# Early value blocks fetched ahead of the first expert row, and six expert chains written as loops

## The chip, the cores and the metric

The kernel runs on one core of a Trainium2 chip. Its time is the device time of one execution in microseconds (us). The core has TensorE (PE; its weight loads are shown as PEld), VectorE (DVE), ScalarE (ACT), GpSimd (POOL) and SyncE (SP), which run their own instruction streams and meet at semaphores, and 16 DMA engines that serve queues filled by SP, ACT and POOL.

## What is computed

Two transformer blocks over 16 meta tokens and 256 real tokens of width 1024. The part that the change touches is the expert layer of the first block:

```python
q = (t @ w_peer_q).reshape(T, PEER_HEADS, 2, PEER_HALF)
s1 = jnp.einsum('thd,hkd->thk', q[:, :, 0], sub_keys1)      # 8 heads, 128 keys
s2 = jnp.einsum('thd,hkd->thk', q[:, :, 1], sub_keys2)
v1, i1 = lax.top_k(s1, PEER_TOPK)                            # 16 of 128, twice
v2, i2 = lax.top_k(s2, PEER_TOPK)
sc, pos = lax.top_k(cand, PEER_TOPK)                         # 16 of the sums v1 + v2
gates = jax.nn.softmax(sc, axis=-1)
...
act = jax.nn.gelu(jnp.einsum('nkd,nd->nk', expert_u[e], xt), approximate=False)
y = jnp.einsum('nk,nkd->nd', g * act, expert_v[e])
```

Every token takes 8 heads times 16 experts, and every expert is a row of 2 x 1024 floats (u and v). The second block begins with projections of the normalised result; its values are `a @ w_in_2[:, values]`.

## The kernel before, in words

Weights come as a stream of 206 blocks of 128 x 1024 floats (512 KB). SP loads block b into slot b % 4 of `ring` as soon as block b - 4 has been split (L432 to L445). ACT rounds a block into `w_hi` (`split_hi`, L356 to L363), DVE writes the rest into `w_lo` (`split_lo`, L365 to L372), and PE multiplies with both. The blocks around the change are 24 to 31 (`w_out`), 32 to 39 (`w_peer_q`), 40 to 47 (`w_in_2_values_0`: the values of the second block's first 128 real tokens and of the meta tokens, here the "early value blocks") and 48 and on (`w_in_2_features`), which wait for the last dot product.

The expert layer runs as 256 rows (SLOTS), in 16 chains of 16 (a chain is one head for one half of the tokens). For row n, with one token on each of the 128 partitions:

- POOL gathers 128 expert rows of 8 KB by index into buffer n % 8 of `gathered` (L510 to L517), 1 MB in all. It waits until PE has used row n - 8 (`row_used`).
- DVE multiplies the u half with the token and sums (`dot`, L2147 to L2159), into a `product` buffer.
- ACT makes gelu, coefficient and a diagonal matrix of it (`coefficient`, L1446 to L1458).
- PE multiplies the diagonal with the v half and adds into PSUM (`add_row`, L938 to L947).

Between the dots DVE works out the experts of later chains: `route_step` has 18 steps for a chain (`STEPS`), and `route_to` spreads them, three for each of the first six rows and about 18/16 for each row after. ACT's `top_exp` and DVE's `gates` make the softmax weights of a chain at its row 12 and rows 14 and 15 of the chain before. The whole row stage is written out, without loops, on every engine; later stages have loops (PE: L1078, L1152, L1156; ACT and DVE have short ones).

Ahead of row 0 ACT's order is: `w_out` and `w_peer_q` splits between `query_hi` pieces, `take_query(0)`, the first scores, further queries and scores, `gain_tokens`, the root, `top_exp(0)`. DVE's is: `route_step(0, ...)`, `first_experts` (which releases the first gathers), and so on. Blocks 40 and 41 are split at rows 48 and 52 (`AHEAD_AT`), blocks 42 to 47 every ten rows from row 170 (`EARLY_AT`), where their tiles are multiplied. As the ring has four slots, block 40 is loaded when block 36 is split, 41 to 43 at rows 0, 1 and 3, 44 and 45 at rows 49 and 53, 46 and 47 at rows 174 and 184.

Of the kernel before, what the change touches and what calls it, by code (L numbers as in the profile page):

```python
# [108 lines left out]
EARLY_AT, EARLY_STEP = SLOTS // 2 + 42, 10  # L109
BANK = [g % 2 if g < TILE0["w_out"] or 0 <= g - TILE0["w_peer_q"] < 8 else g % 2 + 2 if 0 <= g - TILE0["w_in_2_values_0"] < 8  # L110
# [14 lines left out]
def build(nc, stream, rows_dram, small_dram, keys_dram, kiwi_dram, gain_dram, x_dram, gain_rows_dram, meta_2_dram, out_dram):  # L125
    with ExitStack() as ctx:
# [13 lines left out]
        x_hi = sb("x_hi", [P, C * T], F32R)  # L140
# [99 lines left out]
        for name, n in (("qp", PH * REAL), ("sc", CHAINS * 2 * NKEYS), ("v", 2 * TOPK), ("cand", SPREAD),  # L240
                        ("tv", SLOTS), ("gate", SLOTS), ("sum", CHAINS), ("rsum", CHAINS), ("ix", 2 * TOPK),
                        ("pos", TOPK), ("hi", TOPK), ("lo", TOPK), ("af", TOPK), ("bf", TOPK), ("row1", TOPK),
                        ("eq1", TOPK * TOPK), ("eq2", TOPK * TOPK), ("i1", TOPK), ("i2", TOPK),
                        ("expert", SLOTS), ("late", 4), ("dot", SLOTS), ("gelu", SLOTS), ("coef", SLOTS),
                        ("diag", DIAGS * P), ("product", 2 * D), ("scaled", D), ("normed", D), ("stats", 24)):
            route[name] = work[:, base:base + n]
            base += n
        assert base <= WORK, base
        peer_x = (tokens_of(x_peer, REAL), tokens_of(x_lo, REAL))
# [4 lines left out]
        late = route["late"].bitcast(U32)  # L254
        halves_dram = rows_dram.rearrange("e (h n) -> (e h) n", h=2)

# [27 lines left out]
        sq_late = work[:, ROWS * ROW:ROWS * ROW + C * T]  # L284

# [34 lines left out]
        row_landed = [sem(f"row_landed{i}") for i in range(ROWS)]  # L320
        late_chosen, late_landed = sem("late_chosen"), [sem(f"late_landed{i}") for i in range(2)]
# [9 lines left out]
        norm1_landed = sem("norm1_landed")  # L331
# [23 lines left out]
        def split_hi(act, b, turn=None):  # L355

            if b >= BLOCKS:
                return
            t, k = (0, b % RING) if turn is None else (turn, b % RING)
            act.wait_ge(landed[k], t * 16 + 16 * (b // RING + 1))  # L360
            if turn is not None or b >= RING:
                act.wait_ge(block_begun, t * RING + (b - RING + 2))
            nc.scalar.activation(w_hi[:, k, :], ring[:, k, :], ACT.Copy).then_inc(w_hi_ready, 1)  # L363

        def split_lo(dve, b, turn=None):  # L365
# [5 lines left out]
            nc.vector.tensor_tensor(w_lo[:, k, :], ring[:, k, :], w_hi[:, k, :].bitcast(F32),  # L371
# [46 lines left out]
        def _(sp):  # L418
            at = SMALL["norm1"][0]
            sp.dma_start(norm1_gain[:, :], small_dram[:, at:at + C]).then_inc(norm1_landed, 16)  # L420
# [10 lines left out]
            for first, end in ((1, late), (late + 2, BLOCKS // RING)):  # L431
# [5 lines left out]
                if first == 1:  # L437
                    for b in range(late * RING, (late + 2) * RING):
# [113 lines left out]
        AHEAD_AT = {8: 48, 9: 52}  # L552
# [615 lines left out]
        def _(act):  # L1168
# [185 lines left out]

            def query_hi(n):
# [21 lines left out]
            query_hi(0)  # L1377
            split_hi(act, wo + 5)
# [39 lines left out]
            def top_exp(c):  # L1418

                act.wait_ge(tops_shifted, c + 1)  # L1420
                act.wait_ge(peer_rooted, 1)
                g = route["gate"][:, TOPK * c:TOPK * c + TOPK]
                t = c // PH
                a(g, g, ACT.Exp, scale=peer_root[:, t:t + 1],
                  accum_out=route["sum"][:, c:c + 1]).then_inc(tops_exp, 1)

            take_query(0)
            act.wait_ge(first_scores_ready, 1)
# [13 lines left out]
            top_exp(0)  # L1442
# [3 lines left out]
            def coefficient(n):  # L1446

                act.wait_ge(dotted, n + 1)
                t = n // (SLOTS // 2)
                link(a(route["gelu"][:, n:n + 1], route["dot"][:, n:n + 1], ACT.Gelu, scale=peer_root[:, t:t + 1]))  # L1450
                if n % TOPK == 0:
                    act.wait_ge(gates_ready, n // TOPK + 1)
                link(a(route["coef"][:, n:n + 1], route["gelu"][:, n:n + 1], ACT.Copy,  # L1453
# [1171 lines left out]
```

## Time and profile before

| | |
|---|---|
| median of three runs | 1331.97 us (1330.75 to 1331.97) |
| the profiled execution | 1331.13 us, of which 1329.4 us are the span of the trace |
| mean granted TensorE clock | 0.99 |
| busy: PE, DVE, ACT, POOL | 89%, 67%, 51%, 20% of the span |
| DMA | 382.25 MB, mean 288 GB/s over the span |

A profile page gives the busy time of each engine, the span in 40 equal slices (33 us each; a digit is a busy share in tenths), the DMA queues, and the chain of waits followed back from the last instruction. A row of a group or of the timeline names the line of the kernel, the engine, what is written from what, the count and the time; in brackets or behind the bar stands the idle time before it and who ended it. The row stage is the stretch from 191.6 us (first dot) to 837.3 us (end of the last).

### The profile page before, as it was taken

The numbers are of one execution on the slowest core, as the hardware profiler recorded it, in microseconds if no ns is written. First come the engines' busy times: TensorE is split into PE (matmuls) and PEld (weight loads), VectorE is DVE, ScalarE is ACT, GpSimd is POOL, SyncE is SP. The second block draws the span as 40 slices with busy tenths as digits, with TensorE's granted clock in tenths as the row PEclk, the third lists the DMA queues.
The fourth block names the chain that finished last, engine by engine and source line by source line (L and its number), as shares of the span: only waits on it lengthen the run. The fifth ranks groups of instructions, "written<-read, shape, count | busy, mean of one in ns | idle before, by whom it ended". The sixth has DMA issues, their size and how long they took to land.

```text
span 1329.4 us, 19028 instructions
## 1 busy us (share of the span) xinstructions
PE 1187.2 (89%) x6314; PEld 835.7 (63%) x6314; DVE 886.1 (67%) x1939; ACT 683.1 (51%) x1483; POOL 270.9 (20%) x307
## 2 busy tenths in 40 slices
PE   8899989987787878788778878999999999999998
PEld 6898874532222223233333323799999999999986
DVE  6664688666666667776766654666877657666664
ACT  6555655545444345554455544534456675444454
POOL 4000023433333333343333333000000020000000
PEclk9899999999999999999999999999999999999999
DMA  6331389999999999999999999535565355555563
GB/s 240 118 114 64 113 324 419 421 421 420 422 421 422 421 422 420 384 415 422 420 421 421 421 422 413 192 126 190 166 217 188 127 169 181 174 175 183 178 214 101
DMA packets 68939, 382.25 MB, mean 288 GB/s; under 512 B 7792, under 2 KB 7920, under 8 KB 36224
## 3 DMA queue, kind: packets, MB, share of 16 engines
q0 software_dynamic: 37152, 268.45, 48.8%
q1 hardware_dynamic: 31424, 112.05, 25.7%
q10 hardware_dynamic: 288, 0.82, 0.2%
q8 instruction: 39, 0.64, 0.2%
q14 instruction: 36, 0.29, 0.1%
HBM read 380.24 MB, written 1.05 MB: 287 GB/s over the span
## 4 chain that ended last, share of the span: by engine, by line
PE 55%; DMA 31%; ACT 5%; DVE 5%; issue 4%; another core or an unknown queue 0%; SPq 0%; ACTq 0%; DVEq 0%
PE ps L588 31%; DMA work<-in_rows,work 30%; PE ps L943 9%; PE ps L1038 5%; DVE work L2156 1%; ACT work L1457 1%; DVE w_lo L371 1%; PE ps L842 1%; PE ps L621 1%; ACT work L1453 1%; ACT work L1450 1%; PE ps L631 1%; PE ps L622 1%; PE ps L684 1%; PE ps L619 1%
## 5 line engine op out<-in xcount | busy, mean ns | idle before, releaser
L943 PE MATMUL ps<-work 128*128 128x512 f32 x1024 | 496.9, 618 | 120.6 <-ACT work L1457 120.0
L2156 DVE CUSTOM_DVE_ANT_0 work<-work,ps 128x1024 f32<-128x1024 f32 x256 | 312.3, 1220 | 206.6 <-DMA work<-in_rows,work 200.9
L943 PEld LDWEIGHTS ps<-work 128*128 128x128 f32 x1024 | 180.7, 192 | 422.7 <-ACT work L1457 273.2
L514 POOL DMA_INDIRECT work<-in_rows,work x254 | 242.9, 956 | 560.8 <-PE ps L943 391.2
L371 DVE TENSOR_TENSOR w_lo<-ring,w_hi 128x1024 fp32r<-128x1024 f32 x206 | 251.4, 1225 | 112.7 <-ACT w_hi L363 111.0
L588 PE MATMUL ps<-x_lo,w_hi 128*128 128x256 f32 (+2 forms) x1224 | 296.1, 284 | 1.0 <-DVE x_lo L388 0.9
L363 ACT ACTIVATE w_hi<-ring 128x1024 fp32r<-128x1024 f32 x206 | 214.8, 1052 | 55.7 <-PE ps L1038 24.5
L588 PEld LDWEIGHTS ps<-x_lo,w_hi 128*128 128x128 f32 x1224 | 230.8, 192 | 2.8 <-DVE x_lo L388 1.7
L1450 ACT ACTIVATE work<-work,peer_root 128x1 f32<-128x1 f32 x256 | 75.0, 293 | 299.9 <-DVE work L2156 299.7
L588 PE MATMUL ps<-x_hi,w_hi 128*128 128x256 f32 (+2 forms) x760 | 188.1, 291 | 1.6 <-ACT x_hi L381 0.8
L588 PEld LDWEIGHTS ps<-x_hi,w_hi 128*128 128x128 f32 x760 | 141.9, 190 | 6.0 <-issue 3.0
L588 PE MATMUL ps<-x_peer,w_hi 128*128 128x256 f32 x464 | 115.0, 289 | 0.0
L1196 ACT ACTIVATE work<-ps 128x256 f32<-128x256 f32 (+6 forms) x92 | 35.3, 384 | 145.6 <-PE ps L588 125.2
L1457 ACT ACTIVATE work<-ident,work 128x128 f32<-128x128 f32 x256 | 102.8, 401 | 8.4
L588 PE MATMUL ps<-x_hi,w_lo 128*128 128x256 f32 (+2 forms) x760 | 106.5, 282 | 0.0
L588 PEld LDWEIGHTS ps<-x_hi,w_lo 128*128 128x128 f32 x760 | 97.7, 189 | 0.0
L588 PEld LDWEIGHTS ps<-x_peer,w_hi 128*128 128x128 f32 x464 | 88.8, 194 | 1.1 <-issue 0.7
L1453 ACT ACTIVATE work<-work 128x1 f32<-128x1 f32 x256 | 75.3, 294 | 8.4
L588 PE MATMUL ps<-x_peer,w_lo 128*128 128x256 f32 x464 | 65.1, 283 | 0.0
L588 PEld LDWEIGHTS ps<-x_peer,w_lo 128*128 128x128 f32 x464 | 59.8, 192 | 0.0
L548 POOL TENSOR_TENSOR work<-work 128x256 f32<-128x256 f32 x8 | 8.7, 1106 | 240.4 <-ACT work L1664 236.3
L1038 PE MATMUL ps<-w_hi,x_hi 128*128 128x512 f32 x176 | 47.5, 389 | 0.0
(385 smaller groups left out, 1196.3 us busy)
## 6 DMA issues: line engine op xcount, KB each, us to landing
ring<-in_stream SPq DMA_DIRECT2D x206, 512.0 KB, 3.5
work<-in_rows,work POOLq DMA_INDIRECT x258, 15.2
res<-in_tokens SPq DMA_DIRECT2D x4, 272.0 KB, 3.6
gain_rows<-in_gain_rows SPq DMA_DIRECT2D x1, 1024.0 KB, 10.0
out_dram<-work SPq DMA_DIRECT2D x4, 256.0 KB, 2.2
keys_sb<-in_keys SPq DMA_DIRECT2D x1, 512.0 KB, 8.5
work<-in_gain ACTq DMA_DIRECT2D x1, 512.0 KB, 4.3
work<-in_kiwi ACTq DMA_DIRECT2D x1, 288.0 KB, 3.0
```

The costliest lines, as they stand in the source:

```text
L363: nc.scalar.activation(w_hi[:, k, :], ring[:, k, :], ACT.Copy).then_inc(w_hi_ready, 1)
L371: nc.vector.tensor_tensor(w_lo[:, k, :], ring[:, k, :], w_hi[:, k, :].bitcast(F32), ALU.subtract).then_inc(w_lo_ready, 1)
L514: g.indirect_dma_start(out=gathered[:, n % ROWS, :], out_offset=None, in_=rows_dram, in_offset=bass.IndirectOffsetOnAxis(ap=expert[:, n:n ...
L588: last = mm(out, w[:, k, c * P:(c + 1) * P], x[:, c, skip:], start=n == 0, stop=n == 3 * C - 1)
L619: i = mm(out[0:PAIR], x_meta[:, c, :, :], hi, start=c == 0, stop=False)
L943: last = mm(ps[:, Y_BANK[t] + j, :], diag[:, n % DIAGS, :], gathered[:, n % ROWS, D + 512 * j:D + 512 * j + 512], start=False, stop=k == S ...
L1038: last = mm(ps[:, 4 + 2 * t + j, :], x, w[:, k, 512 * j:512 * j + 512], start=False, stop=True, skip_group_check=True)
L1196: a(out, bank_of(g)[0:rows, 0:tokens], ACT.Copy).then_inc(tile_taken[BANK[g]], 1)
L1450: link(a(route["gelu"][:, n:n + 1], route["dot"][:, n:n + 1], ACT.Gelu, scale=peer_root[:, t:t + 1]))
L1453: link(a(route["coef"][:, n:n + 1], route["gelu"][:, n:n + 1], ACT.Copy, scale=route["gate"][:, n:n + 1]))
L1457: a(diag[:, n % DIAGS, :], ident[:, :], ACT.Copy, scale=route["coef"][:, n:n + 1]).then_inc(diag_ready, 1)
L2156: v.tensor_tensor_reduce(R["product"][:, D * (n % 2):D * (n % 2) + D], gathered[:, n % ROWS, 0:D], ps[:, bank:bank + 2, :].rearrange("p b ...
```

## The change

Six of the eight early value blocks (40 to 45, `PARKED`) are not loaded through the ring. ACT issues their loads itself: four (40, 43, 44, 45) between `query_hi(0)` and `split_hi(wo + 5)`, two (41, 42) between `take_query(0)` and the copy of the first scores. They land in buffers that are idle by then: the score table's part for the last chains of each half, the former `x_hi` (now `x_hold`), and 3 x 1024 columns of `work`. SP's loop ends at block 39; blocks 46 and 47 follow as soon as 38 and 39 are split, at rows 1 and 3. Blocks 40 to 43 are split at rows 12, 16, 24 and 28, and blocks 44 to 47 as before.

To make room, per-chain tables shrink to one chain (`tv`, `dot`, `gelu`, `coef`, `sum`, `rsum`), the dot writes its product over the row that it read, and DVE copies a chain's scores into `now` before routing it (`load_scores`). With every chain alike, DVE's rows 32 to 127 (chains 2 to 7) are a loop of six turns, ACT's rows 32 to 111 (chains 2 to 6) a loop of five; its waits count from the loop's register. In the loop, turn i routes chain i + 2, all 18 steps. Before it DVE routes 1.5 steps a row up to 54, and after it `route_to` asks for 181 steps at row 128, where the loop has left 162.

```diff
+EARLY = FIRST["w_in_2_values_0"]
+PARKED = range(EARLY, EARLY + 6)
...
+        parks = [route["sc"].rearrange("p (t n) -> p t n", t=2)[:, :, 6 * 2 * NKEYS:8 * 2 * NKEYS]]
+        parks += [x_hold[:, BLOCK * k:BLOCK * (k + 1)] for k in range(2)]
+        parks += [route["park"][:, BLOCK * k:BLOCK * (k + 1)] for k in range(3)]
...
-            act.wait_ge(landed[k], t * 16 + 16 * (b // RING + 1))
-            if turn is not None or b >= RING:
+            if b in PARKED:
+                act.wait_ge(norm1_and_parked, 16 + 16 * len(PARKED))
+            else:
+                act.wait_ge(landed[k], t * 16 + 16 * (rings_before(b) + 1))
+            if b == PARKED[3]:
+                act.wait_ge(tile_ready, TILE0["w_in_2_values_0"])
+            elif turn is not None or b >= RING:
...
-            for first, end in ((1, late), (late + 2, BLOCKS // RING)):
+            for first, end in ((1, EARLY // RING), (late + 2, BLOCKS // RING)):
...
+                    for b in range(PARKED.stop, late * RING):
+                        sp.wait_ge(w_lo_ready, b + 1 - 2 * RING)
+                        sp.dma_start(ring[:, b % RING, :], stream[b]).then_inc(landed[b % RING], 16)
...
-        AHEAD_AT = {8: 48, 9: 52}
+        AHEAD_AT = {8: 12, 9: 16, 10: 24, 11: 28}
+        LOOP, ACT_LOOP = (2, PH), (2, PH - 1)
...
+            def park(b):
+
+                act.dma_start(raw_block(b), as_parked(b, stream[b])).then_inc(norm1_and_parked, 16)
...
             query_hi(0)
+            for b in (PARKED[0], *PARKED[3:]):
+                park(b)
             split_hi(act, wo + 5)
...
             take_query(0)
+            for b in PARKED[1:3]:
+                park(b)
             act.wait_ge(first_scores_ready, 1)
...
-            def coefficient(n):
+            def coefficient(c, s, t, first=False):
...
+                act.wait_ge(dotted, c * TOPK + (s + 1))
+                gelu, coef = route["gelu"][:, s:s + 1], route["coef"][:, s:s + 1]
+                a(gelu, route["dot"][:, s:s + 1], ACT.Gelu, scale=peer_root[:, t:t + 1]).then_inc(gelu_ready, 1)
...
+                        with act.Fori(*ACT_LOOP) as i:
+                            for k in range(TOPK):
+                                coefficient(i, k, 0)
+                                if k == 12:
+                                    nc.scalar.preload_act_table_set("natural_log_exp_and_others")
+                                    top_exp(i + 1, 0)
+                                    nc.scalar.preload_act_table_set("gelu_and_others")
...
+            def load_scores(c):
+
+                if turn[0] is None and c == 0:
+                    dve.wait_ge(first_scores_taken, 1)
+                else:
+                    dve.wait_ge(key_scores_taken, c % PH + 1 if turn[0] is None else PH)
+                mark(v.tensor_copy(R["now"], sc[:, c, :]))
...
+            def dot(c, s, t):
+
+                dve.wait_ge(row_landed[s % ROWS], c * 32 + 16 * (s // ROWS + 1))
+                bank, u = (6, 0)[t], gathered[:, s % ROWS, 0:D]
                 v.tensor_tensor_reduce(
...
+            def chain_rows(i):
+
+                at, turn[0] = steps[0], i
+                assert routed[0] == STEPS * (LOOP[0] + 1)
+                for s in range(TOPK):
+                    settled()
+                    dot(i, s, 0)
+                    if s == 0:
+                        gates(i, 1)
+                    for step in ((s,), (12, 13), (14,), (15, 16), (17,))[max(0, s - 11)]:
+                        route_step(i + 2, step)
+                    if s == 14:
+                        gates(i + 1, 0)
...
-                route_to(3 * (n + 1) if n < 6 else STEPS // 2 + 10 + (n - 4) * STEPS // TOPK)
-                if c + 1 < CHAINS and s in (14, 15):
-                    gates(c + 1, s - 14)
+                if c < LOOP[0]:
+                    route_to(min(3 * (n + 1) if n < 6 else STEPS // 2 + 10 + (n - 4) * 3 // 2, STEPS * (LOOP[0] + 1)))
+                else:
+                    route_to(STEPS * (LOOP[1] + 2) + (n - TOPK * LOOP[1] + 1) * STEPS // TOPK)
```

## Rows read from the trace of the kernel before

**Rows 1.** The page: DMA by slice, and the queues (q0 gathers, q1 SP's loads).

```profile
DMA  6331389999999999999999999535565355555563
q0 software_dynamic: 37152, 268.45, 48.8%
q14 instruction: 36, 0.29, 0.1%
```

**Rows 2.** The waits: total (us), times, longest one.

```profile
DVE work L2156 <- DMA work<-in_rows,work: 200.9, 223, 2.6
```

**Rows 3.** Windows: stretch (us), busy PE, PEld, DVE, ACT, POOL, clock, DMA share, GB/s.

```profile
155.00:160.00 5.00, 5.00 (x44) 5.00 (x43) 3.43 (x5) 3.68 (x7) 0.00 (x0) 1.00 0.08 12
160.00:165.00 5.00, 5.00 (x44) 5.00 (x43) 4.10 (x7) 4.69 (x9) 0.00 (x0) 1.00 0.80 247
165.00:170.00 5.00, 5.00 (x44) 5.00 (x44) 3.68 (x7) 2.95 (x5) 0.00 (x0) 1.00 0.90 279
170.00:175.00 5.00, 4.43 (x38) 4.14 (x37) 4.96 (x12) 3.61 (x6) 0.00 (x0) 1.00 0.43 124
...
185.00:190.00 5.00, 2.68 (x20) 2.26 (x20) 2.15 (x12) 1.96 (x7) 1.82 (x2) 1.00 1.02 425
...
480.00:500.00 20.00, 15.87 (x32) 5.42 (x32) 13.65 (x38) 8.04 (x25) 7.49 (x8) 1.00 1.01 422
```

**Rows 4.** Timeline of DVE: dots of rows 14, 65 to 67, and 253.

```profile
224.53 1.22 DVE L2156 CUSTOM_DVE_ANT_0 work<-work,ps 128x1024 f32<-128x1024 f32 x1 [0.69 <-DMA work<-in_rows,work]
...
355.71 1.22 DVE L2156 CUSTOM_DVE_ANT_0 work<-work,ps 128x1024 f32<-128x1024 f32 x1 [0.84 <-DMA work<-in_rows,work]
...
359.15 1.22 DVE L2156 CUSTOM_DVE_ANT_0 work<-work,ps 128x1024 f32<-128x1024 f32 x1 [1.54 <-DMA work<-in_rows,work]
...
361.63 1.22 DVE L2156 CUSTOM_DVE_ANT_0 work<-work,ps 128x1024 f32<-128x1024 f32 x1 [0.59 <-DMA work<-in_rows,work]
...
833.54 1.22 DVE L2156 CUSTOM_DVE_ANT_0 work<-work,ps 128x1024 f32<-128x1024 f32 x1 [1.24 <-DMA work<-in_rows,work]
```

**Rows 5.** Timeline of SP: its loads in the row stage; then all ring loads to landing.

```profile
185.12 20.46 SPq L436 DMA_DIRECT2D ring<-in_stream  x4
...
316.61 11.40 SPq L436 DMA_DIRECT2D ring<-in_stream  x2
...
635.60 26.64 SPq L436 DMA_DIRECT2D ring<-in_stream  x2
DMA to landing us min/median/max: 3.2/3.5/8.8
```

**Rows 6.** Windows, as rows 3: between two long dot steps.

```profile
359.10:417.20 58.10, 46.50 (x94) 16.58 (x93) 38.78 (x107) 25.63 (x73) 22.26 (x24) 0.97 1.01 421
```

**Rows 7.** The chain of waits in order of time: start, us, what.

```profile
892.93 92.63 PE ps L588 x768
```

**Rows 8.** Timeline of POOL: the gathers of rows 15, 128 and 149.

```profile
219.41 0.94 POOL L514 DMA_INDIRECT work<-in_rows,work  x1 [3.31 <-PE ps L943]
...
500.39 0.94 POOL L514 DMA_INDIRECT work<-in_rows,work  x1 [2.06 <-PE ps L943]
...
559.42 0.94 POOL L514 DMA_INDIRECT work<-in_rows,work  x1 [7.91 <-PE ps L943]
```

**Rows 9.** Timeline of DVE: the dots of rows 15 and 128.

```profile
227.00 1.22 DVE L2156 CUSTOM_DVE_ANT_0 work<-work,ps 128x1024 f32<-128x1024 f32 x1 [0.27 <-DMA work<-in_rows,work]
...
515.14 1.22 DVE L2156 CUSTOM_DVE_ANT_0 work<-work,ps 128x1024 f32<-128x1024 f32 x1 [0.84 <-DMA work<-in_rows,work]
```

**Rows 10.** ACT: a load issued by it, and its timeline ahead of the first row.

```profile
L1578 ACTq DMA_DIRECT2D work<-in_kiwi x1: 392/392/392, 844.6 to 844.6; - x1
...
170.44 0.51 ACT L1358 ACTIVATE x_peer<-res,small 128x256 fp32r<-128x256 f32 x1 [1.59 <-DVE res L2009]
...
173.75 0.38 ACT L1429 ACTIVATE work<-ps 128x256 f32<-128x256 f32 x1 [0.67 <-PE ps L889]
174.13 1.06 ACT L363 ACTIVATE w_hi<-ring 128x1024 fp32r<-128x1024 f32 x1
```

More of the change, by code:

```diff
@@ L139, in build @@
         w_lo = sb("w_lo", [P, RING, BLOCK], F32R)
-        x_hi = sb("x_hi", [P, C * T], F32R)
+        with nc.sbuf_tensor("x_hi", [P, C * T], F32R) as x_hi:
+            pass
+        x_hold = sb("x_hold", [P, C * T])
         x_lo = sb("x_lo", [P, C * T], F32R)
@@ L248, in build @@
         assert base <= WORK, base
+        route["scaled"], route["normed"] = (sq1[:, D * k:D * (k + 1)] for k in range(2))
+        assert base <= one_at["sq"], base
         peer_x = (tokens_of(x_peer, REAL), tokens_of(x_lo, REAL))
@@ L1541, in _ @@
                     take_scores(4)
-                for b in (8, 9):
+                for b in range(8, 12):
                     if n == AHEAD_AT[b]:
@@ L2131, in route_step, with gates @@
                     mark(v.max_index(pos[:, 8:16], tops[:, 8:16], cand))
[L2132 removed]
+                    ts(gate_of[:, c, :], tops, tops[:, 0:1], None,
                        ALU.subtract).then_inc(tops_shifted, 1)
                 else:
+                    if turn[0] is not None:
+                        settled()
                     decode(c, slice(0, TOPK), step - 11)
[L2137 to L2139 removed]
+                    if step == STEPS - 1 and c < CHAINS - 1 if turn[0] is None else step == STEPS - 1:
+                        load_scores(c + 1)
+            def gates(c, step, first=False):
                 if step == 0:
                     dve.wait_ge(tops_exp, c + 1)
[L2142 removed]
+                    mark(v.reciprocal(R["rsum"], R["sum"]))
                 else:
                     settled()
[L2145 to L2155 removed]
+                    if not first:
+                        dve.wait_ge(coef_ready, c * TOPK)
+                    ts(R["share"], R["power"], R["rsum"], None, ALU.mult).then_inc(gates_ready, 1)
+            def dot(c, s, t):
+                dve.wait_ge(row_landed[s % ROWS], c * 32 + 16 * (s // ROWS + 1))
+                bank, u = (6, 0)[t], gathered[:, s % ROWS, 0:D]
                 v.tensor_tensor_reduce(
[L2157 to L2159 removed]
+                    u, u, ps[:, bank:bank + 2, :].rearrange("p b n -> p (b n)"), 1.0, 0.0, ALU.mult, ALU.add,
+                    R["dot"][:, s:s + 1]).then_inc(dotted, 1)
             def first_experts():
@@ L2194, in first_experts @@
                 stt(expert[:, s], R["i1"][:, s], float(NKEYS), R["i2"][:, s], ALU.mult, ALU.add).then_inc(experts_chosen, 1)
+            load_scores(0)
             for step in range(2):
@@ L2205, in _ @@
                 decode(0, slice(8, TOPK), step)
+            load_scores(1)
             routed = [0]
@@ L2291, in _ @@
                     split_lo(dve, wq + 6 + n // 2)
-                for b in (8, 9):
+                for b in range(8, 12):
                     if n == AHEAD_AT[b] + 1:
```

122 lines of the change are left out of this document (63 added, 59 removed).

## Prediction

> **What bounds the kernel now.** I read the page first. DMA stands at 9 tenths from slice 8 to slice 24, and the gathers' queue q0 alone moves 268.45 MB [rows 1]. Then the waits: DVE's dot waited for a gathered row 223 times out of 256, 200.9 us in all and never longer than 2.6 us [rows 2]. So most rows arrive just after DVE has nothing left to do: the row stage is paced by DMA. The windows confirm it: from 185 us on, the DMA share is 1.0 or more (421 GB/s), while DVE is busy 13.65 of 20 us [rows 3]. A megabyte per row then gives the price of a byte. Two ordinary dots stand 2.48 us apart (359.15, 361.63) [rows 4], so a 512 KB block that shares the stage costs half of that, 1.24 us. A second thing paces the stage. From row 65 to row 66 the step is 3.44 us, 0.96 too long, the dot again waiting for DMA, and the delay is not made up later [rows 4]. I counted ten such steps after row 14, some 23 rows apart. Between two of them DVE ran 107 shown operations and 23 unshown waits, about 130 instructions [rows 6], and the instruction queue q14 moves 0.29 MB in 36 packets, 8 KB each [rows 1]. My reading, an inference, is that DVE's instruction fetch delays one of the 16 DMA engines, and each row waits for the slowest. The account closes nearly: from row 14 (224.53) to row 253 (833.54) are 609.0 us [rows 4]. 239 rows at 2.48 are 592.7, four blocks (two loads near 317 and 328, two near 636 and 662 [rows 5]) 5.0, ten fetches 9.6: 607.3.
>
> **Loads taken out late in the stage.** Before, SP loads eight blocks around the rows: 40 at 185.1, 41 to 43 up to 205.6, then 44 and 45, then 46 and 47 [rows 5]. After it, only 46 and 47 remain, in the places of 42 and 43. So four loads leave the stretch after row 14, where every dot waits for DMA: 4 x 1.24 = 5.0 us. Nothing hides this; it is the firm part of the sum.
>
> **Loads taken out early.** The other two (the places of 40 and 41) are worth 2.5 us only if DMA has other work at once. Row 15 shows how much it has: its gather was issued at 219.41 [rows 8] and its dot began at 227.00 [rows 9], 7.6 us. A gather into an empty queue would take about 0.94 for the issue, 2.48 of transfer and 2.0 of latency (the fastest ring load, 3.2 us [rows 5], less its own 1.24), an estimate of 5.4. So at most 2.2 us can be had before the next gather comes too late. DVE's work ahead of dot 7 grows by one copy of scores (an estimate of 0.24) and one more step (0.36, worked out below), which leaves 1.6. The moved loads also take room elsewhere. In the stretches 155 to 160, 160 to 165, 165 to 170 and 170 to 175 the DMA share is 0.08, 0.80, 0.90 and 0.43 [rows 3]. From ACT's issues at about 158, that leaves 2, 1, 0.5 and 2.9 us free, 6.4 and perhaps half a microsecond more until the gathers start, against 6 x 1.24 = 7.4. About 1.0 spills into the gathers, and 2.5 - 1.0 = 1.5 us remain. I take 1.5, between 0 and 2.5.
>
> **What the moved loads cost where they now stand.** A load issued by ACT takes 0.39 us of its queue [rows 10]. Four in a row are 1.6 us, and behind them are queued the splits of blocks 29 to 35 and `query_hi(1)` to `(7)`. `query_hi(7)` waited 1.59 us for DVE [rows 10], and it needs PE's last `w_out` tile anyway, so I cost them at nothing; without that cover, the first rows would come 1.6 us later. The other two, 0.8 us, stand before the copy of the first scores, which was idle for 0.67 us [rows 10]: 0.1. `load_scores(0)` adds about 0.3 ahead of `first_experts`. The first gathers come 0.4 us later, into a queue that still has the spilled 1.0 to do, so it isn't counted twice. SP's ring loads (32 to 37) share DMA with 2 MB more; they land up to 2.5 us later, and PE reaches those blocks 5 us or more after their splits. Nothing.
>
> **More work in rows 6 to 31.** Four splits on ACT (1.06 us each [rows 10]) and four on DVE come to rows 12 to 29, and by row 28 DVE has routed 8 more steps than before. DVE's steps cost 0.36 us each by the windows: 13.65 us in 20, less 8 dots of 1.30 with their read-out, over 9 steps [rows 3]. Per row that is 1.30 + 1.5 x 0.36 + 0.3 for splits, 2.1 us, under 2.48. ACT is not near its limit. This shortens the queue and takes nothing from DMA as long as it never runs dry: 0, with 4.2 us (four splits in a row on the path) as the other end.
>
> **Row 128.** The loop ends with 162 steps routed, and 181 are asked for: 19 steps on DVE after dot 128, about 7 us, with the score copy. Dot 129 would come some 5.6 us late. Row 128 had been issued at 500.39 [rows 8] and its dot began at 515.14 [rows 9], 14.7 us: less the 5.4 of an empty queue, the stage tolerates 9.3 us. The old kernel shows that such a gap passes: before the gather at 559.42, POOL waited 7.91 us for ACT's table loads and roots [rows 8], and dots lost about 0.5. I take -0.5 for everything of this kind; down to -3.
>
> **The loops.** Register waits cost DVE and ACT an operation of some 0.04 to 0.1 us each; both have idle time in every row. What counts is code. Straight, 96 rows take 96 x 130 / 23, 540 instructions, 4.2 packets. As a loop, a turn is about 130: per row two for the dot, one register operation and one wait (64), the chain's 40, and some 25 for gates, register waits and the branch. If a turn's code stays on the engine, 4.2 fetches go away, at most 4.0 us. But ACT and PE fetch too, on other DMA engines by the absence of steps at their pace, and these may stand just behind DVE's; the gain then ends at the next slowest. I take 0.5, between 0 and 4.0.
>
> For staying, one row speaks: in PE's loops of the second block 768 matmuls ran in 92.63 us as one piece [rows 7], 0.12 us each, through eight loop bodies of 96 products, with no stall at a branch. DVE may hold less than PE.
>
> The Trainium skill ("Runtime: NRT & Kernel Launch", section on instruction fetch mechanics) speaks against the change: the instruction memory is refilled in blocks, prefetch is purely sequential, and a taken branch to code outside a window of two blocks forces a fetch before the engine goes on. It gives DVE blocks of 256 instructions; the trace here has packets of 8 KB at a pace of about 130 instructions, so the trace disagrees on the size. By its sizes a turn would fit and the gain above stands; by its rule with the trace's size the turn spans two or three blocks and is fetched anew each time.
>
> **Sum.** 5.0 + 1.5 - 0.5 + 0.5 = 6.5 us. The profiled execution of 1331.13 would become 1324.6. The median of the runs is 0.84 above it, so 1325.5.
>
> **Rivals.** A measurement can tell about 0.2%, 2.7 us, from no change.
>
> (a) *The turn is fetched anew.* DVE's loop crosses packet borders and the branch back finds its code gone. With two fetches a turn it has 12 in place of 4.2: 7.8 x 0.96 = 7.5 us against 6.0, so 1333.5, no change. With three (or ACT's on top) 18: 13.2 us, so 1339.2, slower. It decides from 13 fetches in six turns (6.0 + 2.7 over 0.96, plus 4.2). For it: a turn is about the size of one packet, so it can't lie within one unless aligned. Against it: PE's loops. Two fetches 0.08, three 0.09.
>
> (b) *The first 30 rows are paced by the engines, not by DMA.* The chain from DVE over ACT to PE already sets when row 15 is gathered (POOL waited 3.31 us for PE [rows 8]). With the added splits it falls behind and DMA runs dry: 4.2 us of the gain go, 1329.7. Against it: DMA never dropped below 1.0 there. 0.10.
>
> (c) *The burst at row 128 or a stall at the branches drains the queue*: 3 us more, 1328.5. 0.05.
>
> (d) *The loads are not out of the way.* They crowd the ring loads at 158 to 175 us, PE waits for a block and row 0 comes 3 us later, 1328.5: the bytes are moved in place but not in time. 0.05.
>
> **Numbers.** The forecast has 0.60, its own range 1322.5 to 1328. What is left of 0.03 is other losses. Faster: 0.60 + 0.05 + 0.05 = 0.70. Same: (b) and (a) with two, 0.18. Slower: (a) with three, and the rest, 0.12. The range goes down to 1322 (six whole loads, 7.4, and 2.5 of fetches) and up to 1333.9, which takes in (b), (c), (d) and (a) with two fetches.
>
> **What would show it.** SP's loads in the stage fall from eight to two; the dots between rows 32 and 127 lose their long steps (or get several a turn, each within some rows of a branch); the time from the first dot that waits for DMA to row 253 falls by about 5.5 us; the first dot stays at 191 to 193 us; after row 128 there is a run of 19 steps with no DMA wait behind it for more than ten rows. I am wrong if q14 grows, if DMA shows a gap between rows 8 and 30, or if the waits of rows after 128 last longer than 3 us.

## The result, and the profile after

| | before | after |
|---|---|---|
| median of the runs | 1331.5 us | 1322.55 us (1322.34 to 1323.44) |
| ratio, with its 95% interval | | 0.9936 (0.9921 to 0.9951) |
| span of the trace | 1329.4 us | 1320.4 us |
| mean granted TensorE clock | 0.99 | 0.987 |

The change makes the kernel 9.0 us faster. Measured again, the same code had the ratio 0.9949 (0.9936 to 0.9962), 6.8 us by the medians of that chip; the two intervals together reach from 5 to 10.5 us. The forecast was 6.5 us. The sign holds, and so does the range, though only just (1322.55 where it began at 1322). But several of its terms are wrong, in opposite directions.

The page of the kernel after; the slices are 33 us each:

```profile
DMA  6332499999999999999999999545565356555562
GB/s 245 118 112 65 160 350 390 422 422 421 422 421 422 421 421 409 405 421 421 421 422 421 421 421 416 195 134 186 163 233 174 117 181 183 164 183 182 178 215 100
q10 hardware_dynamic: 1280, 3.97, 0.9%
q14 instruction: 29, 0.24, 0.0%
```

Beside [rows 1], the instruction queue has 29 packets, not 36. q10 carries ACT's loads; before it had 0.82 MB, so the parked 3.15 MB are there. The DMA share still looks full in slice 7 (198 to 231 us), but the rate is 390 GB/s there, where the kernel before has 419. That is the first hint of a loss at the start of the rows.

The waits of DVE (total us, times, longest), and SP's loads from 150 to 900 us:

```profile
DVE work L2213 <- DMA work<-in_rows,work: 182.4, 200, 1.9
...
199.99 5.67 SPq L471 DMA_DIRECT2D ring<-in_stream  x2
827.76 16.02 SPq L476 DMA_DIRECT2D ring<-in_stream  x8
```

The dot waits for its row 200 times, where [rows 2] has 223: the row stage is still paced by DMA. SP's loads in it are down from the eight of [rows 5] to two (those from 827.76 us on belong to the next stage).

The dots of rows 32, 128, 129 and 253 in DVE's timeline, first that of row 32 before, then after:

```profile
270.18 1.22 DVE L2156 CUSTOM_DVE_ANT_0 work<-work,ps 128x1024 f32<-128x1024 f32 x1 [0.76 <-issue]
```

```profile
269.84 1.22 DVE L2213 CUSTOM_DVE_ANT_0 work<-work,ps 128x1024 f32<-128x1024 f32 x1 [1.26 <-DMA work<-in_rows,work]
...
508.87 1.22 DVE L2213 CUSTOM_DVE_ANT_0 work<-work,ps 128x1024 f32<-128x1024 f32 x1 [0.97 <-DMA work<-in_rows,work]
...
519.48 1.20 DVE L2213 CUSTOM_DVE_ANT_0 work<-work,ps 128x1024 f32<-128x1024 f32 x1
...
824.00 1.22 DVE L2213 CUSTOM_DVE_ANT_0 work<-work,ps 128x1024 f32<-128x1024 f32 x1 [1.27 <-DMA work<-in_rows,work]
```

With [rows 4] and [rows 9] these split the gain. Up to row 32 it is 0.34 us (270.18 to 269.84). From row 32 to row 128 it is 5.93 us (244.96 before, 239.03 now, which is 96 rows at 2.49 with no long step). From row 128 to row 253 it is 3.27 us (318.40 to 315.13). The rest of the program takes 496 us in both.

The first stretch hides a loss. This is the chain of waits (start, us, what; pieces left out) ahead of the rows, first before, then after:

```profile
147.33 0.86 PE ps L794 x2
...
172.70 0.39 ACT work L1196
```

```profile
145.81 0.86 PE ps L829 x2
...
157.45 1.07 ACT w_hi L394
...
159.94 6.95 DMA ring<-in_stream
166.91 1.07 ACT w_hi L394
...
173.21 0.40 ACT work L1231
```

L794 is L829 after (I call this point P, the last norm matmuls), and L1196 is L1231 (point Q, the first query tile). From P to Q the kernel before takes 25.37 us and the kernel after 27.40. The 2.03 us more are a ring load that is late behind the parked loads; before, PE ran through. That P itself stands 1.5 us earlier is no work of the change: it lies between 145.8 and 148.5 us in executions whose code up to there is alike, so I measure from P.

### The profile page after: what moved, and what is told of

It is laid out like the page before. It is cut to its first block, busy times and chain, and to the rows that moved or that the text cites. A ratio compares the mean times of both kernels' runs of the same rounds, so it can differ in the third digit from the quotient of the medians.

```text
span 1320.4 us, 19083 instructions
## 1 busy us (share of the span) xinstructions
PE 1187.4 (90%) x6314; PEld 836.8 (63%) x6314; DVE 889.7 (67%) x1955; ACT 685.5 (52%) x1483; POOL 270.7 (21%) x307
## 3 DMA queue, kind: packets, MB, share of 16 engines
HBM read 380.24 MB, written 1.05 MB: 289 GB/s over the span
## 4 chain that ended last, share of the span: by engine, by line
PE 59%; DMA 24%; ACT 7%; DVE 6%; issue 3%; another core or an unknown queue 0%; ACTq 0%; SPq 0%; DVEq 0%; POOLq 0%
PE ps L623 30%; DMA work<-in_rows,work 23%; PE ps L978 14%; PE ps L1073 5%; ACT work L1499 2%; DVE work L2213 2%; DVE w_lo L402 1%; ACT w_hi L394 1%; DMA ring<-in_stream 1%; PE ps L656 1%; PE ps L877 1%; PE ps L666 1%; PE ps L657 1%; ACT work L1495 1%; ACT work L1491 1%
## 5 line engine op out<-in xcount | busy, mean ns | idle before, releaser
L978 PEld LDWEIGHTS ps<-work 128*128 128x128 f32 x1024 | 183.9, 193 | 409.5 <-ACT work L1499 250.5
L548 POOL DMA_INDIRECT work<-in_rows,work x254 | 242.5, 955 | 551.5 <-PE ps L978 379.4
L402 DVE TENSOR_TENSOR w_lo<-ring,w_hi 128x1024 fp32r<-128x1024 f32 x200 | 244.0, 1226 | 115.8 <-ACT w_hi L394 114.2
L394 ACT ACTIVATE w_hi<-ring 128x1024 fp32r<-128x1024 f32 x200 | 208.8, 1054 | 58.1 <-PE ps L1073 24.5
L1231 ACT ACTIVATE work<-ps 128x256 f32<-128x256 f32 (+6 forms) x92 | 35.5, 386 | 146.2 <-PE ps L623 125.1
```

The lines of the kernel that those rows point to most:

```text
L394: nc.scalar.activation(as_parked(b, w_hi[:, k, :]), raw_block(b), ACT.Copy).then_inc(w_hi_ready, 1)
L402: nc.vector.tensor_tensor(as_parked(b, w_lo[:, k, :]), raw_block(b), as_parked(b, w_hi[:, k, :].bitcast(F32)), ALU.subtract).then_inc(w_lo ...
L548: g.indirect_dma_start(out=gathered[:, n % ROWS, :], out_offset=None, in_=rows_dram, in_offset=bass.IndirectOffsetOnAxis(ap=expert[:, n:n ...
L978: last = mm(ps[:, Y_BANK[t] + j, :], diag[:, n % DIAGS, :], gathered[:, n % ROWS, D + 512 * j:D + 512 * j + 512], start=False, stop=k == S ...
L1231: a(out, bank_of(g)[0:rows, 0:tokens], ACT.Copy).then_inc(tile_taken[BANK[g]], 1)
```

## The experiments

For each kernel the table has the ratio to the kernel before on its chip, and from its one profiled execution the time from P to Q, from P to the dot of row 32, from 32 to 128, from 128 to 253, and the packets of q14 (the first from the chain or ACT's timeline, the dots from DVE's). One execution is no exact measure: of the two pairs of executions of the same code, one differs by 0.4 us from P to row 253 (after), the other by 1.7 (the parked loads moved apart).

| kernel | ratio | P to Q | P to 32 | 32 to 128 | 128 to 253 | P to 253 | q14 |
|---|---|---|---|---|---|---|---|
| before | 1 | 25.4 | 122.9 | 245.0 | 318.4 | 686.2 | 36 |
| after | 0.9936 | 27.4 | 124.0 | 239.0 | 315.1 | 678.2 | 29 |
| after, measured again | 0.9949 | 27.4 | 125.5 | 238.7 | 314.5 | 678.6 | 30 |
| ring | 0.9977 | 25.4 | 127.2 | 240.1 | 314.6 | 681.9 | 29 |
| straight | 0.9972 | 27.5 | 127.2 | 240.4 | 314.3 | 681.9 | 35 |
| dve_straight | 0.9972 | 27.8 | 124.9 | 242.5 | 314.6 | 682.0 | 33 |
| act_straight | 0.9932 | 27.6 | 122.4 | 239.3 | 315.6 | 677.3 | 31 |
| pad8 | 0.9950 | 28.5 | 123.2 | 240.5 | 314.5 | 678.2 | 30 |
| straight_pad8 | 1.0006 | 28.2 | 123.9 | 247.1 | 314.5 | 685.6 | 41 |
| spread | 0.9946 | 27.8 | 124.8 | 239.3 | 314.1 | 678.2 | 29 |
| parks_split | 0.9922 | 25.4 | 120.8 | 239.6 | 314.8 | 675.2 | 29 |
| parks_split_b | 0.9924 | 25.4 | 122.7 | 239.1 | 315.1 | 676.9 | 29 |
| split_spread_b | 0.9926 | 25.4 | 122.2 | 239.2 | 314.5 | 675.9 | 29 |
| parks_late_b | 0.9952 | 25.4 | 124.3 | 239.7 | 314.6 | 678.6 | 29 |

**No loads parked.** All eight early value blocks go through the ring; the loops stay.

```
-PARKED = range(EARLY, EARLY + 6)
+PARKED = range(EARLY, EARLY)
...
-                        sp.wait_ge(w_lo_ready, b + 1 - 2 * RING)
+                        sp.wait_ge(w_lo_ready, b + 1 - RING)
...
-            for b in (PARKED[0], *PARKED[3:]):
-                park(b)
...
-            for b in PARKED[1:3]:
-                park(b)
```

> The changed kernel with all eight early value blocks through the ring again, at the rows where it splits them (40 to 43 loaded as before, 44 to 47 at rows 13 to 29); the loops stay. Theory now: of the six loads only those that fall where dots wait for DMA count. The places of blocks 40 and 41, ahead of row 8, lie where the gathers are issued too late to use them, so 0.3 us, and four at 1.24 give 5.0: 5.3 us slower than the changed kernel, 1327.9. Rival, every load counts: 7.4 us, 1330.0. Rival, the loops made the gain and the loads nothing: 1323 or less.

Measured: 1327.68 us, 0.9977 (0.9965 to 0.9988). The time is the one that the theory gave, but by other terms. P to Q is back at 25.4 us, so the parked loads do cost 2 us there. And beside the kernel before, which also has its eight loads in the rows, this one gains 4.3 us from P to row 253. The loops are the first candidate, but this kernel also keeps the change's other work in the rows (the copies of the scores, the other order of routing, the place of four splits), so the next three test them.

**Both loops written out**, the parked loads kept.

```
-                        with dve.Fori(*LOOP) as i:
+                        at0 = steps[0]
+                        for i in range(*LOOP):
+                            steps[0], routed[0] = at0, STEPS * (LOOP[0] + 1)
...
-                        with act.Fori(*ACT_LOOP) as i:
+                        for i in range(*ACT_LOOP):
```

> The changed kernel with both loops written out, same order of work, same loads. Theory: DVE's instruction fetches come back in rows 32 to 127, about four long dot steps of 3.44 us, 0.96 us each: 3.5 to 4 us slower than the changed kernel, 1326.3. Rival, the next slowest DMA engine caps it (as the prediction had it): 0.5 us, 1323.1. Rival, the loops gave nothing: 1322.6.

**Only DVE's loop written out** (the first of these two edits).

> The changed kernel with DVE's loop written out, ACT's left. Theory, it is DVE's fetches: the same as with both written out, 1326.3, and four long steps. Rival, it is ACT's fetches: 1322.6 and none.

**Only ACT's loop written out** (the second).

> The changed kernel with ScalarE's loop written out and VectorE's loop kept. With VectorE's loop alone written out the time rose from 1322.6 to 1327.7 us, and with both written out it was the same 1327.5. Theory, only VectorE's instruction fetches cost time (the long dot steps stand at multiples of some 128 VectorE instructions), ScalarE's fall beside a queue that is not at its limit: 1322.6 us, and no dot step over 3.1 us in rows 32 to 127. Rival, each engine's fetches cost, and the second one's are hidden only while the first one's are there: 1326 to 1328 us, with long steps in these rows.

Measured: 1327.51 us, 0.9972 (0.9963 to 0.9982); 1327.65, 0.9972 (0.9963 to 0.9982); 1320.92, 0.9932 (0.9919 to 0.9945). The loops are worth 0.0023 to 0.0036 of the time, 3.1 to 4.8 us, and all of it is DVE's. On the chip of the first two of these three kernels the version with the routing spread (below) had 0.9946 with both loops, 0.0026 less. ACT's loop saves packets too (q14 has 31 without it, 29 with it) and no time. Where DVE's is written out, the long steps are back. These are the dots of rows 91 and 92 in it:

```profile
421.66 1.22 DVE L2213 CUSTOM_DVE_ANT_0 work<-work,ps 128x1024 f32<-128x1024 f32 x1 [0.83 <-DMA work<-in_rows,work]
...
425.11 1.22 DVE L2213 CUSTOM_DVE_ANT_0 work<-work,ps 128x1024 f32<-128x1024 f32 x1 [2.05 <-DMA work<-in_rows,work]
```

The step is 3.45 us, as that of row 66 in [rows 4], and there are four such in rows 32 to 127 (47, 69, 92, 115; the first is 3.29 us). The view of the queues in a window says what stands in a step. First the step above (421.66 to 425.11 us), then 315 to 505 us (some 75 of these rows) in this kernel, then in the kernel after, where q14 doesn't appear at all:

```profile
q14 instruction: 1, 0.01, 0.6%
...
q14 instruction: 3, 0.02, 0.0%
...
q0 software_dynamic: 10999, 80.11, 101.3%
q8 instruction: 2, 0.03, 0.1%
```

All four long steps hold a packet of q14, and so do the ten that the prediction counted in the kernel before. ACT's packets do nothing of the kind: with ACT's loop written out, they stand in rows 70 and 99, and the steps are 2.48 and 2.49 us. PE's (q8) stand in rows 73 and 105 of every kernel, in steps of 2.47 to 2.54 us; but one in row 42 of the spread kernel (below) stands in a step of 3.32, so PE's may cost something at times. With both loops written out only two of the long steps show (92, 115), though the whole is as slow. DVE's packets stand in the two other places too, but the steps there are 2.49 and 2.46 us; that execution lost its time ahead of row 32, where its transfers ran at 363 to 378 GB/s. So a fetch doesn't cost the same each time. Why not, no run shows.

Nor does a loop remove every fetch: its first turn still has DVE's packet in row 44. In the kernel after that step is 2.81 us, in the first version with the parked loads apart 3.46.

**Longer code in the loop, and the dose.** Eight one-column memsets behind each dot of chains 2 to 7, once in the loop, once with both loops written out.

```
+        idle = sb("idle", [P, 24])
...
                 for s in range(TOPK):
                     settled()
                     dot(i, s, 0)
+                    for j in range(8):
+                        v.memset(idle[:, j:j + 1], 0.0)
```

> The changed kernel with eight one-column memsets on a tile of their own behind every dot of VectorE's loop, 128 more instructions in a turn and 768 more executed; extra work, nothing is left out. A turn then covers twice as many instructions as before. Theory, a turn of this size still stays where it was fetched: no fetches in the loop, and as VectorE has 0.7 us to spare in each row of 2.49 us and eight memsets of some 0.06 us take 0.5, 1322.6 to 1323.6 us. Rival, only a turn of some 130 instructions stays and a longer one is fetched at every turn: 6 turns with 2 fetches each at 0.96 us, 1334 us, and the instruction queue has 12 packets more than the changed kernel's 29.

> The same eight memsets behind every dot of chains 2 to 7, with both loops written out: the dose for the price of a fetch. Against the kernel with both loops written out (1327.5 us) VectorE runs 768 instructions more in these rows, 6 more fetches of some 128 instructions. Theory, a fetch in the run that the transfers bound costs 0.96 us: 1333.3 us, 10 to 12 long dot steps in rows 32 to 127. Rival, the loops' gain is not the fetches but something else in the loop's code: no more than 1328.5 us, the memsets alone.

Measured: 1323.48 us, 0.9950 (0.9937 to 0.9964), and 1331.75 us, 1.0006 (0.9996 to 1.0016). The same executed instructions cost 7.4 us more, from P to row 253, when they are written out. In windows of the two looped kernels, the one after and then the one with the memsets (busy PE, PEld, DVE, ACT, POOL, clock, DMA share, GB/s), 128 more operations of DVE stand in the same 40 us:

```profile
412.00:452.00 40.00, 31.44 (x65) 11.07 (x65) 27.15 (x75) 18.83 (x52) 15.27 (x17) 1.00 1.01 422
```

```profile
412.00:452.00 40.00, 32.55 (x65) 11.94 (x66) 29.15 (x203) 18.72 (x53) 15.23 (x17) 0.96 1.01 422
```

They add 2.0 us of busy time and nothing to the pace of the rows here. (Over all of rows 32 to 127 this kernel takes 1.5 us more than the one after; both its long steps, 3.38 and 3.44 us, stand in the first turn, with a packet of q14 each.) So a turn of some 260 instructions, about two packets' worth, isn't fetched anew: q14 has 30 packets, where two a turn would have made 41, and none of them lies between 315 and 505 us. Written out, the same memsets bring q14 from 35 to 41, the predicted six. The dots of rows 76 and 77, and of rows 85 and 86, in that kernel:

```profile
383.92 1.22 DVE L2214 CUSTOM_DVE_ANT_0 work<-work,ps 128x1024 f32<-128x1024 f32 x1 [0.97 <-DMA work<-in_rows,work]
...
387.36 1.22 DVE L2214 CUSTOM_DVE_ANT_0 work<-work,ps 128x1024 f32<-128x1024 f32 x1 [1.37 <-DMA work<-in_rows,work]
...
407.23 1.22 DVE L2214 CUSTOM_DVE_ANT_0 work<-work,ps 128x1024 f32<-128x1024 f32 x1 [0.59 <-DMA work<-in_rows,work]
...
410.70 1.22 DVE L2214 CUSTOM_DVE_ANT_0 work<-work,ps 128x1024 f32<-128x1024 f32 x1 [1.78 <-DMA work<-in_rows,work]
```

Both steps are long (3.44 and 3.47), now nine rows apart and not 23. A window over these nine rows counts 117 operations of DVE; with nine unshown waits of the dots that is 126 instructions, as the 130 of [rows 6]:

```profile
387.37:410.63 23.26, 17.60 (x38) 6.05 (x37) 17.17 (x117) 10.83 (x31) 8.43 (x9) 1.00 1.02 422
```

Rows 32 to 127 have nine long steps, eight of them with a packet of DVE in them (the ninth, 3.25 us, has no packet of q14, but one of PE's in the row before), and take 4.6 us more than with DVE's loop alone written out. For six fetches more that is 0.77 us each; by the ratios it is 4.5 us (1.0006 less 0.9972), 0.75 each. So the cost follows the number of fetches, and the long steps are DVE's instruction fetches: 0.96 us where one shows in full, some 0.75 on average. By which way a fetch holds up a row (one of the 16 DMA engines, as the prediction infers) isn't shown.

**The routing after row 128 spread out**, so that the 18 steps of chain 9 don't stand in one piece behind the loop.

```
-                    route_to(STEPS * (LOOP[1] + 2) + (n - TOPK * LOOP[1] + 1) * STEPS // TOPK)
+                    route_to(STEPS * (LOOP[1] + 1) + (n - TOPK * LOOP[1] + 1) * STEPS // TOPK)
```

> The changed kernel with DVE's 19 steps at row 128 taken apart: routing goes on at 18 steps per 16 rows from where the loop left it. Theory: the burst drained the gathers' queue (from row 128 to row 140 took 31.5 us where 12 rows at 2.48 are 29.8), so 1.7 us faster than the changed kernel, 1320.9. Rival, the queue bore it as the prediction had it (9.3 us of slack): no change, 1322.6.

Measured: 1323.76 us, 0.9946 (0.9929 to 0.9963), where 1320.9 us had been expected. Rows 128 to 253 are 1.05 us shorter than in the first execution of the kernel after, and 0.4 shorter than in its second. In the kernel after, dot 129 stands 10.61 us behind dot 128 and carries no wait for DMA. These are its windows from 525 us on, and then those of the spread kernel (columns as above):

```profile
525.00:530.00 5.00, 5.00 (x10) 2.00 (x9) 5.00 (x14) 3.29 (x9) 1.88 (x2) 0.80 0.83 300
530.00:535.00 5.00, 5.00 (x13) 2.28 (x12) 4.97 (x13) 2.70 (x9) 2.81 (x3) 1.00 1.01 372
```

```profile
525.00:530.00 5.00, 4.10 (x9) 1.37 (x9) 4.10 (x10) 1.98 (x6) 1.91 (x3) 1.00 1.01 415
530.00:535.00 5.00, 4.14 (x10) 1.40 (x9) 3.34 (x10) 1.98 (x6) 1.93 (x3) 1.00 1.01 419
```

The burst lets the gathers run out: in these ten microseconds 0.8 MB aren't moved, some 2 us of transfer. Half of it or less is lost for good. In the whole it is too small to be told.

**The parked loads moved apart.** The last two of the first four are issued behind a later split, from 167.80 us on, some 10 us later than in the changed kernel.

```
-            for b in (PARKED[0], *PARKED[3:]):
+            for b in (PARKED[0], PARKED[3]):
                 park(b)
...
             split_hi(act, wq + 2)
+            for b in PARKED[4:]:
+                park(b)
```

> The changed kernel with two of the four first parked loads (the fifth and sixth parked blocks) issued some 14 us later, behind ScalarE's split of the third w_peer_q block, where the transfers have room; the other four stay where they were. In the changed kernel the chain of waits has 6.95 us of a ring load at 159.9 us that lands late, and the stretch from the last norm tile at 145.8 us to the first x tiles at 171.6 us is 1.7 us longer than in the kernel that parks nothing. Theory, the four parked loads crowd this ring load: the stretch shrinks by 1.0 to 1.7 us and the time is 1321.0 to 1321.6 us. Rival, the first row's time is set by something else (the granted clock near 190 us, the gathers): the time stays 1322.6 us within 0.5.

> The changed kernel itself, on the chip of the next three, as their reference: the ratio to the kernel before stays at 0.9936 within 0.0012. If its first measurement flattered it, 0.9950 or more.

> The version with the last two of the first four parked loads issued some 14 us later, once more beside the changed kernel. Theory, the 2.04 us that its chain from the last norm tile to the first query tile is shorter come through in full: 1.5 to 2.0 us below the changed kernel of the same chip. Rival, the 1.9 us of its first measurement were a difference between chips: within 0.5 us of the changed kernel.

Measured: 1320.42 us, 0.9922 (0.9909 to 0.9935); then, on one chip, the changed kernel 1323.87, 0.9949 (0.9936 to 0.9962), and this one again 1320.51, 0.9924 (0.9911 to 0.9937). The changed kernel came out between the two outcomes expected of it (0.9936 and 0.9950). This one beats it by 1.9 us by the first two ratios and by 3.4 us on the same chip, more than the 2.0 of the theory. Its chain has no DMA any more, and P to Q is 25.37:

```profile
147.59 0.86 PE ps L829 x2
...
172.96 0.39 ACT work L1231
```

Its first execution gains more than these 2.0 us from P to row 253 (3.0 against the kernel after), and windows from 200 to 230 us say why. First before, then after, then this kernel:

```profile
200.00:215.00 15.00, 12.34 (x38) 4.97 (x37) 14.69 (x47) 6.06 (x19) 5.34 (x5) 1.00 1.02 420
215.00:230.00 15.00, 14.62 (x56) 7.64 (x55) 12.54 (x38) 11.07 (x29) 6.57 (x7) 1.00 1.01 416
```

```profile
200.00:215.00 15.00, 12.60 (x33) 5.14 (x32) 14.66 (x46) 5.47 (x16) 4.86 (x5) 0.91 1.01 395
215.00:230.00 15.00, 13.95 (x56) 7.45 (x54) 13.60 (x42) 11.13 (x27) 6.53 (x7) 1.00 1.00 380
```

```profile
200.00:215.00 15.00, 12.18 (x44) 6.14 (x43) 14.73 (x49) 6.48 (x20) 5.35 (x5) 1.00 1.02 419
215.00:230.00 15.00, 13.25 (x38) 5.80 (x37) 13.70 (x41) 11.52 (x29) 6.27 (x7) 1.00 1.02 423
```

The kernel after moves 0.025 x 15 + 0.036 x 15 = 0.9 MB less than before in these 30 us, 2.2 us of transfer. The first eight gathers are issued soon after Q; the next wait until PE has used rows 0 and on, and that begins with the first dot. My reading is that the time from Q to the first dot counts. In the kernel after it is 18.55 us (173.21 to 191.76), and the chain has an unexplained wait of 3.96 us in it (last section). In this kernel it is 15.26 us (172.96 to 188.22), without that wait, and the transfers stay full. The ninth gather shows it; in POOL's timeline, first of the kernel after and then of this one, it waited for PE:

```profile
197.15 0.94 POOL L548 DMA_INDIRECT work<-in_rows,work  x1 [9.00 <-PE ps L978]
```

```profile
193.54 0.94 POOL L548 DMA_INDIRECT work<-in_rows,work  x1 [5.87 <-PE ps L978]
```

The second execution of the same code had the wait, 19.05 us (172.40 to 191.45), and 383 and 404 GB/s; it lost 1.9 us from P to row 32 against the first. The kernel with ACT's loop written out had no such wait (15.3 us) and 418 and 421 GB/s. The kernel before and the one without parked loads had the wait (18.9 us both) and full transfers all the same: two further ring loads filled the gap. All fourteen traces fit this. In the four without the wait the two windows have 411 to 423 GB/s; in the three with the wait and further loads behind Q (before, ring, parks_late_b) 416 to 424; in the seven with the wait and no such loads 363 to 404. The granted clock, 0.91 in the one window above, isn't what decides: from 190 to 200 us it is 0.83 in the kernel before and in the one with ACT's loop written out too, and both have full transfers. So these loads were worth little where they stood, and the place of the parked ones is a cost of its own, 2.0 us.

**Both edits together.**

> The version with the two later parked loads, and behind row 128 VectorE's 18 routing steps start a chain later, so that the burst of 10.6 us at row 129 is gone. Alone the second edit took 1.05 us out of rows 128 to 253 and nothing measurable out of the whole. Theory, both gains are in stretches that the transfers bound, one after the other, and add: 0.5 to 1.0 us below the version with the later loads alone. Rival, the burst costs nothing that isn't lost elsewhere: within 0.4 us of it.

Measured: 1320.84 us, 0.9926 (0.9912 to 0.9939), as with the parked loads moved alone. The 0.5 to 1.0 us that the theory gave can't be seen.

**All six loads behind the first query tile.**

```
-            for b in (PARKED[0], *PARKED[3:]):
-                park(b)
...
             take_query(0)
-            for b in PARKED[1:3]:
+            for b in PARKED:
                 park(b)
```

> All six parked loads are issued in one row behind the first query tile, where two stood. Theory, nothing crowds the ring loads any more and the 2.04 us come back, but ScalarE's four more issues of 0.41 us stand ahead of its copy of the first scores, on which VectorE's first routing and the first gathers wait, 1.6 us, and four loads of 1.24 us now share the DMA engines with the first gathers, up to 5 us: 1.5 to 4 us above the version with the two later loads. Rival, only the crowding of the ring loads counts and the transfers have room behind it: as that version within 0.5 us.

Measured: 1324.7 us, 0.9952 (0.9938 to 0.9966). P to Q is short again (25.4), and the first dot comes at 194.2 us: 20.7 us behind Q, where the version with two later loads had 19.05 on that chip. It is 4.2 us slower than that version: the theory holds in kind, slightly above its upper end of 4. So it counts where the loads go: two into the empty stretch of [rows 3] at 155 us, two into the one at 170, and not all six just ahead of the gathers.

## Why the prediction was right and where it wasn't

**The bound and the price of a byte: right.** The rows are paced by DMA, 2.48 us each, and a block costs 1.24. Between the kernel without parked loads and the one with them well placed lie 6.7 and 5.0 us from P to row 253 (its two executions), and 7.2 us by the ratios (0.9977 less 0.9923, the mean of its two). Six blocks at 1.24 are 7.4.

**Four late loads, 5.0 us: right as far as it was tested.** Rows 32 to 253 gain 9.2 us. With DVE's loop written out 6.2 us of them stay (563.4 us before, 557.1): the 5.0, and 1.2 that no term stands for. No run moved these four loads alone.

**Two early loads, 1.5 us: 0.3 to 0.9 came.** The step that failed is "1.0 spills into the gathers, and 2.5 - 1.0 = 1.5 us remain", which let DMA have work at every moment. It had none to spare: the missing 0.9 MB are 2.2 us, and 2.5 less 2.2 is 0.3. From Q to the dot of row 32 the trace gains 0.85 (97.48 us before, 96.63 now), the second execution loses 0.54. The slack of 2.2 us was read at row 15. What ran out was the ninth gather, which waited 9.00 us for PE. This is rival (b), at half its size and with another cause. The engines fall behind not by the added splits, which the version with the loads apart has too, at 419 and 423 GB/s, but because the first row comes late behind its gathers. And that is in part luck: in the four traces without the unexplained wait the stretch from Q to row 32 is 1.8 to 2.7 us shorter than before.

**What the moved loads cost, "Nothing": wrong by 2.0 us.** The failed step is "PE reaches those blocks 5 us or more after their splits". I had taken that margin for the blocks on average; the ring load at 159.94 landed only 6.95 us later, ACT's split waited for it, and the chain went through it. Nor were the loads "up to 2.5 us later": the one issued 11.5 us behind P took 7.3 us to land, where before it took 3.4. This is rival (d), with 2.0 us where it said 3, and I gave it 0.05. "The first dot stays at 191 to 193 us" came true (191.76) only because P was 1.5 us early in that execution.

The Trainium skill ("DMA: Bandwidth & Descriptors", section on queues, rings and completion order) says that each DMA engine takes turns between the queue rows that have work for it. Four loads on ACT's queue would then share every engine with the ring loads that SP issues after them. The trace of the kernel after agrees as far as it shows the sharing; the turns themselves can't be seen in it. ACT issued its four from 155.07 us on, SP's late load was issued at 159.94, and a window over the 7 us to its landing is full from end to end:

```profile
160.00:167.00 7.00, 7.00 (x60) 7.00 (x60) 4.52 (x7) 5.12 (x9) 0.00 (x0) 1.00 1.01 406
```

**Row 128, -0.5 us: right in kind, -0.4 to -1.05 in size.** Dot 129 came 10.6 us behind dot 128, a gap of 8.1 us and not 5.6. It lies within the bound of -3 and passes, as POOL's wait of 7.91 us in [rows 8] did.

**The loops, 0.5 us: the term that was mis-sized.** They brought 3.1 to 4.8 us by the ratios, and 3.8 in the traces from P to row 253 (682.0 less 678.2). The count of fetches and their price were nearly right (4.2 at 0.96, at most 4.0 us): of DVE's four in rows 32 to 127 three are gone, and the one of the first turn cost little. The step that failed is "the gain then ends at the next slowest": it set ACT's and PE's fetches just behind DVE's, with no row for it but caution. The kernel with ACT's loop written out has two packets more and loses nothing. The upper end of the term was the right value, and rows that show ten steps of one engine's pace and none of another's had said so.

**Rival (a), the turn fetched anew: refuted.** q14 fell from 36 to 29, and even a turn of some 260 instructions stayed. The Trainium skill ("Runtime: NRT & Kernel Launch", section on instruction fetch mechanics) states that a taken branch outside the current two blocks forces a fetch. The traces agree as far as they go: the branch back over 260 instructions was still inside, which fits two blocks of the size that the page gives (256 instructions) and not two of the packets here (some 130). So the prediction's reading "by its rule with the trace's size" is what failed; longer turns weren't tried.

**The sum: luck in part.** It held by errors that nearly cancel: 2.6 to 4.3 us too little for the loops, 2.0 too much for the place of the parked loads, and some 1 too much for the early ones. With the measured terms it would be 6 to 8 us. The trace has 8.0 from P to row 253, of which about 1 us has no term; the other 1.0 of the 9.0 is the early P (1.5) less 0.5 us behind row 253.

**The signs.** The loads, the vanished long steps, row 128 (no dot waits for DMA until row 139) and q14 came as said. "If DMA shows a gap between rows 8 and 30" came true in part: the share stayed at 1.00, but the rate fell to 380 GB/s. The first dot that waits for DMA is now that of row 25 and not of row 14, and from there to row 253 the gain is 9.2 us (580.8 to 571.6) where about 5.5 was forecast.

## What to carry to other kernels

Where a stream of transfers sets the pace, count the long steps and what one engine executed between two of them. If the count is constant, suspect instruction fetches, look for the queue's packet in the window of a long step, and write that engine's rows as a loop: here it removed all but the fetches of the first turn. Bytes taken out of a full stretch pay in full only if they go where the queue is empty and no critical load is issued behind them. Look at the stretch ahead in windows of a few microseconds, and split the loads over the gaps. A filler that is removed uncovers a late start of the consumer: watch GB/s, not only the share, at the head of the stage.

## What the runs showed that I had not expected

- A fetch of DVE's instructions cost 0.75 us on average in the full stretch and 0.96 where it showed in full, a fetch of ACT's nothing measurable, though both are on q14 (31 packets against 29, ratio 0.9932 against 0.9936).
- The DMA share can't tell a slightly starved stretch: it was 1.00 at 380 GB/s and 1.02 at 423.
- The first dot stood between 188.2 and 195.8 us in kernels that gave medians within 0.6% of each other, and in two executions of one code at 188.22 and 191.45. In ten of the fourteen traces the chain ahead of it holds some 3 to 4 us of waiting, on ACT or at PE's issue, that nothing in the profile explains; in four it isn't there (ACT's loop written out, both kernels with memsets, the first execution with the parked loads apart). In the kernel after:

```profile
185.27 3.96 another core or an unknown queue
189.25 0.39 ACT work L1231
```

In nine of the ten traces 16 products of PE with the identity (L967) come in pieces in these same microseconds, in the kernel after from 185.53 to 189.87, while DVE and POOL go on; in the other five traces they run in one piece of 2.03 us. What ends this wait stays open; no run was aimed at it. It is also why the stretch ahead of row 32 differs by 2 us between executions of one code.
